# Layer 0 of a hybrid attention/convolution backbone: five stages ahead of attention become one stage over blocks of 512 tokens

## What is computed

```python
shift, scale, gate = split(silu(c) @ w_mod[0] + b_mod[0], 3)    # for the latents (c) and for the context (c_ctx)
h = rms_norm(x, g_pre[0]) * (1 + scale) + shift                # 2048 latent rows and 256 context rows
u = h @ w_in                                                   # 1024 -> 384 (q latent), 256 (kv latent), 64 (rotary key), 1024 (gate)
q  = rms_norm(cq,  g_q)  @ w_uq                                # 384 -> 8 heads x (128 + 64 rotary)
kv = rms_norm(ckv, g_kv) @ w_ukv                               # 256 -> 8 heads x (128 key + 128 value)
q_rope, k_rope = rope_2d(q_rope), rope_2d(kr)                  # latents only
```

## Time and profile before

| | us |
|---|---|
| median of 3 runs (lowest, highest) | 3414.61 (3414.49, 3419.63) |
| the profiled execution, its time | 3415.36 |
| its span, first to last instruction | 3413.6 |
| end of the last product ahead of attention, within the span | 753.3 |

### The profile page before, as it was taken

The page is one execution under the profiler, slowest core; times in us unless marked ns, Lnnn a source line. Parts: engine busy times, 40 slices in busy tenths (PEclk is TensorE's granted clock), DMA queues, the critical chain, the costliest instruction groups (busy, mean ns, idle before and its releaser), DMA issues. The chain is left out here.

```text
span 3413.6 us, 44910 instructions
## 1 busy us (share of the span) xinstructions
PE 3101.9 (91%) x15389; PEld 2570.4 (75%) x15389; DVE 1655.4 (48%) x2781; ACT 1350.1 (40%) x2896; POOL 432.8 (13%) x285
## 2 busy tenths in 40 slices
PE   7699979687999999999999999797699999997798
PEld 7588857466888787878787888686588888886677
DVE  0501134326676767676767676532533333332554
ACT  1412123345555555555555555422411111111543
POOL 1200000001111111111110111000311111112331
PEclk9799989898999999999999999999799999998899
DMA  5212133552121212121111110343322222212442
GB/s 167 82 67 74 65 108 126 174 219 90 38 66 38 67 38 66 38 66 38 62 41 53 43 38 19 136 148 116 103 70 68 70 70 70 70 51 92 158 146 101
DMA packets 216850, 285.77 MB, mean 84 GB/s; under 512 B 80560, under 2 KB 143424, under 8 KB 215488
## 3 DMA queue, kind: packets, MB, share of 16 engines
q1 hardware_dynamic: 212032, 274.76, 24.5%
q10 hardware_dynamic: 4608, 8.39, 0.7%
HBM read 185.04 MB, written 98.05 MB: 83 GB/s over the span
## 5 line engine op out<-in xcount | busy, mean ns | idle before, releaser
L988 ACT ACTIVATE at_prob<-at_S,at_nmax 128x512 f32<-128x512 f32 (+1 forms) x640 | 411.0, 658 | 373.9 <-DVE at_nmax L1102 373.9
L1125 DVE TENSOR_TENSOR at_ptlo<-at_T,at_pthi 128x512 fp32r<-128x512 f32 x576 | 396.5, 688 | 320.7 <-ACT at_pthi L1004 317.7
L1004 ACT ACTIVATE at_pthi<-at_T 128x512 fp32r<-128x512 f32 x576 | 348.9, 608 | 224.5 <-PE at_T L874 224.5
L1091 DVE TENSOR_REDUCE at_mx<-at_S 128x1 f32<-128x512 f32 (+1 forms) x640 | 393.4, 629 | 79.7 <-PE at_S L848 69.3
L874 PE MATMUL at_T<-ident,at_prob 128*128 128x128 f32 x2304 | 346.4, 273 | 1.7 <-DVE at_ptlo L1125 1.7
L874 PEld LDWEIGHTS at_T<-ident,at_prob 128*128 128x128 f32 x2304 | 278.9, 140 | 67.6 <-DVE at_ptlo L1125 13.7
L95 PE MATMUL ci_ps<-h1hi,ci_whi 128*128 128x512 f32 x768 | 299.7, 390 | 17.5 <-DVE ci_wlo L1553 17.5
L96 PE MATMUL ci_ps<-h1lo,ci_whi 128*128 128x512 f32 x768 | 299.3, 390 | 0.0
L97 PE MATMUL ci_ps<-h1hi,ci_wlo 128*128 128x512 f32 x768 | 299.3, 390 | 0.0
L843 PE MATMUL at_S<-at_khi,at_qhi 128*128 128x512 f32 (+1 forms) x640 | 250.1, 391 | 49.5 <-ACT at_prob L988 26.1
L95 PE MATMUL at_O<-at_pthi,at_vhi 128*128 128x512 f32 x576 | 272.8, 474 | 0.6 <-DVE at_og L1134 0.5
(11 more groups left out here) (201 smaller groups left out, 6293.1 us busy)
## 6 DMA issues: line engine op xcount, KB each, us to landing
at_wmod<-in_w_mod SPq DMA_DIRECT2D x32, 512.0 KB, 3.6
ci_w<-in_cv_w_in SPq DMA_DIRECT2D x24, 512.0 KB, 4.3
values<-kvu_ob SPq DMA_DIRECT2D x36, 256.0 KB, 2.0
at_kst<-k_nope SPq DMA_DIRECT2D x8, 1152.0 KB, 7.7
at_vst<-values SPq DMA_DIRECT2D x8, 1152.0 KB, 8.0
mod_w<-in_w_mod SPq DMA_DIRECT2D x16, 512.0 KB, 3.5
hid_x<-in_x SPq DMA_DIRECT2D x16, 512.0 KB, 5.2
silu_gate<-inp_ob SPq DMA_DIRECT2D x32, 256.0 KB, 2.3
```

The lines of the kernel that those rows point to most:

```text
L988: nc.scalar.activation(prob[:, j % 2, i, k], S[:, c, 0:k.stop - k.start], ACT.Exp, scale=SCALE, bias=nmax[:, i % 2:i % 2 + 1], accum_out=l ...
L1004: nc.scalar.activation(dst, T[:, (n + SLOTS * j) % 2], ACT.Copy).then_inc(s_hi, 1)
L1091: nc.vector.tensor_reduce(mx[:, i % 2, c:c + 1], S[:, c, 0:k.stop - k.start], AXX, ALU.max).then_inc(s_mx, 1)
L1125: nc.vector.tensor_tensor(ptlo[:, kt % 3], T[:, (n + SLOTS * j) % 2], pthi[:, kt % 3].bitcast(F32), ALU.subtract).then_inc(s_lo, 1)
```

## The change

`modulation`, `in_proj` and `latents` go; `front` takes their place and that of the call of `hidden` for layer 0. It is one block with no barrier inside.

- **Modulation** moves to VectorE: `w_mod` is stored transposed, `silu(c)` is broadcast over the partitions, and 32 `scalar_tensor_tensor` operations of 128x1024 with an accumulated sum give the 16 tiles for the two streams. Seven buffers of 512 KB take the weights. The first block's row statistics are done meanwhile.
- **Tokens outside, weights inside.** For each block of 512 latent tokens the 24 chunks of the list `ORDER` pass by: R0 to R5 (the latent tiles and the rotary key), G0 to G7 (the gate), U0 to U5 (two query outputs each), K0, K1 (four key outputs each), V0, V1 (four value outputs each). Each chunk (512 KB; U 384 KB) is loaded and split again for each block, in two raw buffers and three split ones, two steps ahead. The last block follows `ORDER_END`, with three chunks C3 to C5 more for the context (99 steps in all).
- **The next block's `h`** is made beside it: transposes of one eighth after each of eight steps (`T_AFTER`), into two PSUM banks; the split parts have two slots.
- **Latents stay in SBUF** and are normalised in the same block: column sums after R0 (kv) and G0 (q), roots at R1 and G1. `raw_latents` is neither written nor read.
- **Gate**: one `Silu` on ScalarE in the eviction. **Rotary**: VectorE reads PSUM itself; a `stream_shuffle` swaps the halves, three more operations combine them.

```diff
-def modulation(nc, net):
...
+RAWS, GATES, QS, KEYS, VALS = (tuple(f"{n}{i}" for i in range(k)) for n, k in (("R", 6), ("G", 8), ("U", 6), ("K", 2), ("V", 2)))
+CHUNKS = RAWS + GATES + QS + KEYS + VALS
+ORDER = ("R3 R4 R5 R0 R1 R2 G0 G1 K0 G2 K1 G3 V0 G4 V1 U0 U1 U2 G5 U3 U4 G6 U5 G7").split()
+ORDER_END = ("R3 R4 R5 R0 R1 R2 G0 C3 C4 C5 G1 G2 K0 G3 K1 V0 V1 U0 U1 G4 U2 U3 G5 U4 U5 G6 G7").split()
+T_AFTER = ("G0", "G1", "K0", "G2", "K1", "G3", "V0", "G4")
+T_AFTER_END = ("R3", "R4", "R5", "R0")
+SHUFFLE = [(i + ROPE // 4) % (ROPE // 2) for i in range(ROPE // 2)]
...
+def front(nc, net):
...
+        hhi, hlo = sb("hhi", [P, 2, KD, BLK], F32R), sb("hlo", [P, 2, KD, BLK], F32R)
+        xt = sb("x", [P, R, D])
+        tmp = sb("tmp", [P, 2, BLK])
+        wst = sb("w", [P, 2, D])
+        whi, wlo = sb("whi", [P, 3, D], F32R), sb("wlo", [P, 3, D], F32R)
...
+            load_x(0)
+            for i in range(MOD_FIRST):
+                if i >= MR:
+                    sp.wait_ge(s_mdot, 2 * (i - MR + 1))
+                sp.dma_start(mwst[:, i % MR], net.w_modr[i]).then_inc(s_mw[i % MR], 16)
+            load_w(0)
+            load_w(1)
...
+            for g, (t, name) in enumerate(seq):
+                if g + 2 < NG:
+                    sp.wait_ge(s_wlo, g + 1)
+                    load_w(g + 2)
+                if name == "R3":
+                    if t:
+                        sp.wait_ge(s_rope, 5 * t)
+                    for i in range(2):
+                        sp.dma_start(cs[:, i], net.rope_tab[i, :, t * BLK:(t + 1) * BLK]).then_inc(s_cs, 16)
+                    if t == 0:
+                        sp.wait_ge(s_T, KD)
+                        load_x(1)
+                if name == "U0" and t + 2 < len(hid):
+                    sp.wait_ge(s_T, (t + 2) * KD)
+                    load_x(t + 2)
+                if g:
+                    stores(g - 1)
+            stores(NG - 1)
...
+            for k in range(KD):
+                transposes(0, k)
+            for g, (t, name) in enumerate(seq):
+                hs, ws = t % 2, g % 3
+                pe.wait_ge(s_wlo, g + 1)
+                if name[0] in "KVU":
+                    pe.wait_ge(s_xlo, 5 * t + (5 if name[0] == "U" else KKV))
+                for o, (kind, i, e, w, ctx) in enumerate(outs[g], first_out[g]):
+                    if o >= 4:
+                        pe.wait_ge(s_evd if by_dve[o - 4] else s_eva, evicted[o - 4])
...
+                if name == "R0":
+                    column_sum(t, "kv")
+                if name == "G0":
+                    column_sum(t, "q")
+                if t == LAST:
+                    if name in T_AFTER_END:
+                        for k in range(2):
+                            transposes(t + 1, 2 * T_AFTER_END.index(name) + k)
+                    if name == "G1":
+                        column_sum(t, "c")
+                elif name in T_AFTER:
+                    transposes(t + 1, T_AFTER.index(name))
...
+            def w_high(g):
+                n = width_of(seq[g][1])
+                act.wait_ge(s_w[g % 2], 16 * (g // 2 + 1))
+                if g >= 3:
+                    act.wait_ge(s_out, first_out[g - 2])
+                nc.scalar.activation(whi[:, g % 3, 0:n], wst[:, g % 2, 0:n], ACT.Copy).then_inc(s_whi, 1)
...
+                if name == "R0":
+                    square(t, "kv")
+                if name == "R1":
+                    root(t, "kv")
+                if name == "R2":
+                    latent_high(t, "kv")
+                if name == "G0":
+                    square(t, "q")
+                if name == ("C3" if t == LAST else "G1"):
+                    root(t, "q")
+                if name == ("C5" if t == LAST else "K0"):
+                    latent_high(t, "q")
...
+                        dst, func = ob[:, b % 4, 0:w], ACT.Silu if kind == "G" else ACT.Copy
+                    nc.scalar.activation(dst, ps[:, o % 4, 0:w], func).then_inc(s_eva, 1)
...
+            def rotate(u, src, read):
+                if u >= 2:
+                    dve.wait_ge(s_rst[u % 2], 16 * (u // 2))
+                if u:
+                    dve.wait_ge(s_rope, u)
+                nc.vector.stream_shuffle(t2[:], src, SHUFFLE).then_inc(s_rob, 1)
+                nc.vector.tensor_tensor(rob[:, u % 2], src, cs[:, 0], ALU.mult).then_inc(read, 1)
+                dve.wait_ge(s_rob, 2 * u + 1)
+                nc.vector.tensor_tensor(t2[:], t2[:], cs[:, 1], ALU.mult).then_inc(s_rob, 1)
+                dve.wait_ge(s_rob, 2 * u + 2)
+                nc.vector.tensor_tensor(rob[:, u % 2], rob[:, u % 2], t2[:], ALU.add).then_inc(s_rope, 1)
...
+            for i in range(MOD_FIRST):
+                dve.wait_ge(s_mw[i % MR], 16 * (i // MR + 1))
+                if i == 2:
+                    inverse(0)
+                for s in range(2):
+                    if i:
+                        dve.wait_ge(s_mdot, 2 * i + s - 1)
+                    nc.vector.scalar_tensor_tensor(out=mjunk[:, s], in0=mwst[:, i % MR], scalar=1.0, in1=cb[:, s],
+                                                   op0=ALU.mult, op1=ALU.mult,
+                                                   accum_out=msum[:, i, s:s + 1]).then_inc(s_mdot, 1)
+            dve.wait_ge(s_mdot, 2 * MOD_FIRST)
+            nc.vector.tensor_tensor(mod[:, 0:MOD_FIRST], msum[:],
+                                    net.bm[:, 0:MOD_FIRST].unsqueeze(2).to_broadcast([P, MOD_FIRST, 2]),
+                                    ALU.add).then_inc(s_mod, 1)
+            dve.wait_ge(s_mod, 1)
+            scale_rows(nc, net, 0, 2).then_inc(s_amul, 1)
+            w_low(0)
+            for k in range(KD):
+                split_hidden(0, k)
+            w_low(1)
...
-def in_proj(nc, net, hhi, hlo):
...
-def latents(nc, net, kind):
...
-        modulation(nc, net)
-        with ExitStack() as st:
-            hhi = st.enter_context(nc.sbuf_tensor("h0hi", [P, KD, TOK], F32R))
-            hlo = st.enter_context(nc.sbuf_tensor("h0lo", [P, KD, TOK], F32R))
-            hidden(nc, net, 0, net.x, net.ctx, hhi, hlo)
-            in_proj(nc, net, hhi, hlo)
-        latents(nc, net, "q")
-        latents(nc, net, "kv")
+        front(nc, net)
```

More of the change, by code:

```diff
@@ L299, in _ @@
                             t.then_inc(s_tile, 1)
-def in_proj(nc, net, hhi, hlo):
[L304 to L389, removed]
-                act.wait_ge(s_out, o + 1)
-                if o >= 4:
-                    act.wait_ge(s_st[o % 4], 16 * (o // 4))
-                nc.scalar.activation(ob[:, o % 4, 0:width], ps[:, o % 8, 0:width], ACT.Copy).then_inc(s_free, 1)
-            def pair(i, last):
-                for r in range(2):
-                    if not (last and r):
-                        w_high(act, i, RAW + r + 1)
-                    for b in range(NBLK):
-                        o = NRAW + 4 * r + b
-                        act.wait_ge(s_out, i * 8 + (o + 1))
-                        act.wait_ge(s_free, i * 8 + (o - 1))
-                        nc.scalar.activation(sig[:, b % 2], ps[:, o % 8], ACT.Sigmoid).then_inc(s_sig, 1)
-            with act.Fori(0, HEADS // 2 - 1) as i:
-                pair(i, False)
-            pair(HEADS // 2 - 1, True)
-        @block.vector
-        def _(dve):
-            for m in range(RAW + 1):
-                w_low(dve, 0, m)
-            def pair(i, last):
-                for r in range(2):
-                    if not (last and r):
-                        w_low(dve, i, RAW + r + 1)
-                    for b in range(NBLK):
-                        o = NRAW + 4 * r + b
-                        dve.wait_ge(s_sig, i * 8 + (4 * r + b + 1))
-                        dve.wait_ge(s_st[o % 4], i * 32 + 16 * (o // 4))
-                        nc.vector.tensor_tensor(ob[:, o % 4], ps[:, o % 8], sig[:, b % 2],
-                                                ALU.mult).then_inc(s_free, 1)
-            with dve.Fori(0, HEADS // 2 - 1) as i:
-                pair(i, False)
-            pair(HEADS // 2 - 1, True)
@@ L2039, in constants @@
             rows = slice(a * half + h * half // 2, a * half + (h + 1) * half // 2)
-            tab[0, rows, :SEQ], tab[1, rows, :SEQ] = np.cos(ang[a]), np.sin(ang[a])
-    perm = np.zeros((P, P), np.float32)
-    for m in range(P):
-        if m % half < half // 2:
-            perm[m + half // 2, m] = -1.0
-        else:
-            perm[m - half // 2, m] = 1.0
+            tab[0, rows, :SEQ], tab[1, rows, :SEQ] = np.cos(ang[a]), (2 * h - 1) * np.sin(ang[a])
     mask = (np.arange(P)[:, None] // PHASES == np.arange(CCH)[None, :]).astype(np.float32)
-    return {"rope_tab": np.tile(tab, (1, 2, 1)), "perm": perm, "mask": mask, "ident": np.eye(P, dtype=np.float32)}
+    return {"rope_tab": np.tile(tab, (1, 2, 1)), "mask": mask, "ident": np.eye(P, dtype=np.float32)}
 def layout(i):
```

645 lines of the change are left out of this document (404 added, 241 removed).

## The result

The median is **3263.24 us** (3262.19 to 3265.23, 4 runs) against 3414.55 of the kernel before in the same session (3412.73 to 3419.63): ratio 0.9555, 95% interval 0.9539 to 0.9572. That is 151 us less. The forecast was 109 less, 3306, with 3280 as the lowest end. The profiled execution took 3262.19, 1.05 under the median; its span is 3260.2.

A forecast was written before the change was run, and what follows sets the result against it. TensorE, busy 91%, bounds the kernel, so the end of the last product ahead of attention decides: 80.8 + 555.2 + 8 = 644.0 instead of 753.3, 109.3 less, giving 3306 us; own range 3285 to 3325, widened to 3280 to 3345.

The forecast's parts named there:

- Lead-in: Start of the new stage: loads, 32 dots, normalising and splits, until TensorE can run without a gap from 80.8 us.
- Transposes: TensorE's transposes, now between products: 28 groups of four with one change of kind, 1.26 us each, 35.2 in all.
- Column sums: Nine float32 sums on TensorE between products at 1.20 us each (0.85 passes, 0.35 change of kind): 10.8.
- Up-projections: K, V and U on TensorE: 816 matmuls priced at 0.233 us each, 190.4; 0.227 kept for the low end.
- Stalls: TensorE's waits in the new stage: late first transposes 3, R0's column sum 3, dense context steps 2, together 8 us.
- Switches of ScalarE: Table loads between roots and `Silu`, 1.283 us each; a further drain of about 1.4 each would add 7 us.
- The tail: Stores, barrier and attention's loads after the last product: taken as unchanged.
- Rival 1: New stage: all covers hold, no stalls, accumulation free, 0.227 in the up-projections: 3286, or 3284 with faster loads; chance 0.08.
- Rivals 2 and 3: New stage's weights arrive late: short steps lengthen, 3336, chance 0.20; or landings of 12 us make it slower, 3470, chance 0.04.
- rival 2: Weights land late in short steps, at 8 us, so ScalarE's high parts wait: 28 us on U steps, 3336; chance 0.20.
- Rival 4: The stage ends earlier, but attention's start gives it back, by later stores or another clock: no change; chance 0.02.

The follow-up runs named there:

- b_moddve: Kernel before with only the modulation changed, to 32 dots on VectorE, still a stage of its own: 3415.24 us, ratio 1.0004.
- a_tr2: Kernel after with every transpose issued twice, the same piece into the same place: 3277.26 us, ratio 0.9604.
- a_dma2: Kernel after with 97 of the 99 weight chunks loaded a second time into a buffer nobody reads: 3272.34 us, ratio 0.9593.
- b_shuffle: Kernel before with only the 21 permutes on TensorE replaced by a shuffle on VectorE: 3395.17 us, ratio 0.9943.
- b_mdpad64: Kernel before with modulation as VectorE dots and 64 extra unused two-column matmuls on TensorE beside them: 3415.3 us, ratio 1.0008.
- b_mdpad32: Kernel before with modulation as VectorE dots and 32 extra unused two-column matmuls on TensorE beside them: 3394.38 us, ratio 0.9947.

## Why the prediction was right in kind and wrong in size

**Lead-in, "80.8".** Measured 69.6 for the start of the second output, 11.2 less. The first dot started at 16.9, not 18.2. "32 x 1.478 = 47.3" was the larger part of the error: a dot takes 1.15, 10.6 less in all. I took the upper bound "as accumulation always costs a read in this trace", but that read was ScalarE's, one engine's figure for another's operation. b_moddve has the same 1.15. Against this, the two normalisations took 2.4 instead of 1.9, and the dot at 27.33 took 2.04. From bias and scale on (57.2 instead of 68.0) little was gained, though the hidden splits took 1.06 instead of 1.29: "The first output, R3, is paced by those splits" was wrong. TensorE's program has all eight groups of transposes ahead of the first product; the last group starts at 63.63, and only then do the 24 products run, without a gap, past the end of the splits at 66.96. That the splits of before were slower because GpSimd worked beside them was not tested.

**Transposes, "35.2".** This is the step that failed most: "26 in 5.90, 0.227 each. Four and one change of kind are 1.26". Measured 0.48, 28 x 0.48 = 13.4: 21.8 us. Both parts of the price were wrong. The transposes of the earlier trace rows ran at half pace: about 12 of the 21.8. The same stage of the kernel before has both prices. In these windows of L294's instructions (stretch, busy PE and PEld, clock, DMA share, GB/s) the first row is the stretch of the earlier trace rows, the other two come a little later, under a recorded clock:

```profile
78.80:83.80 5.00, 5.00 (x25) 4.85 (x23) 1.00 0.75 215
98.60:101.20 2.60, 2.60 (x14) 2.60 (x14) 0.50 0.45 135
101.50:102.50 1.00, 1.00 (x12) 0.97 (x10) 1.00 0.68 123
```

From start to start these are 0.213, 0.213 and 0.11 us. The clock's record of that trace begins at 84.3; the 1.00 of the first stretch is the print of a missing record. The last stretch has the price that was needed, and I didn't look for it. Attention's 2304 transposes, too, have rows of 273 ns, where those of the earlier trace rows have 421. The other part, "0.35 the change of kind", 28 times 0.35 or 9.8 us, came from the permute's row. There TensorE starts the permute 0.50 after the product before, where 0.23 were due, with the wait put down to "issue"; it is not what a change of kind costs. In the kernel after, four transposes cost 0.48 with both changes, and four times the 0.117 of a_tr2 is 0.47.

I gave this term no lower bound, and so the range had none either: with 13.4 in place of 35.2 the forecast would have been 3284, and the measured dots would have brought it to 3274.

**Column sums, "10.8".** 0.86 each, 3.1 less: the four passes that the forecast had at 0.85, and again no 0.35 for the change of kind, neither with transposes behind the sum nor between products.

**Up-projections, "0.233".** I count them at 0.227, the low end I had kept: 5.4 less. Why the kernel before has 0.233 there (weight loads of 191 ns against 188 to 189) stays open.

**Stalls, "8".** 603.3 less 69.6 is 533.7; the work is 555.2 - 21.8 - 3.1 - 5.4 = 524.9; 8.8 are left, of which 5.9 have a name in the waits. The size was right, but by luck: of the causes that I had worked out, late transposes (3) and R0's square (3) show no wait at all, and the dense context steps (2) show 1.4: 0.78 for `fr_wlo` right behind them, at 505.41, and 0.56 for the context's column sum (`fr_sum`), at 511.71. The rest is the late loads in and beside the query steps (2.2), one eviction at 439.02 (1.5) and the rotation (0.8), where I had counted on full cover.

**Switches of ScalarE.** Each table load took 1.283, as in the earlier trace rows, and where the next activation waited for nothing else it began 0.02 later (17.10 and 1.28, then 18.40):

```profile
17.10 1.28 ACT L90 ACT_TABLE_LOAD   x1
...
18.40 0.30 ACT L90 ACTIVATE fr_rx<-fr_sx,eps 128x4 f32<-128x4 f32 x1
```

The drain that the Trainium skill (ScalarE: Activation LUTs, "What ACT_TABLE_LOAD costs") adds does not appear in this row, and the 7 us that it would have added are not there: no wait of TensorE stands at G1 in the first three blocks.

**The tail** was left as it was, rightly: 23 us in both. **Rival 1** had the right direction but too few bounds in it. **Rivals 2 and 3** did not come true, and a_dma2 with half as much traffic again did not bring them about; but rival 2's chain is there, at 2.2 us, by stores ahead on SP, as its text had said. **Rival 4**, at 0.02, was the most underrated. In the change itself it cost nothing, as attention took 1372.0, and that was luck: three of my runs (b_shuffle, b_moddve, b_mdpad64) show that this could not be counted on, since there attention gave back 8 to 18 us.

The sum of the corrections: 11.2 + 21.8 + 3.1 + 5.4 = 41.5, less 0.8 of stalls, is 40.7: 644.0 becomes 603.3. The remaining 2 us between forecast and result lie behind attention. (By its own working the forecast should have read 3305.3: 109.3 less than the median of 3414.61. The 3306 is 109.3 less than the profiled execution.)

## What to carry over

Before a price is taken from a row, look for the same operation's fastest instance in the trace and for the clock it had, and give every term a lower bound as well as an upper one: here the largest error was in the term that had none. When a change ends its stage earlier and the total doesn't move, compare the length of the unchanged stage behind it before you doubt the change: where it is a long loop, instructions added or removed ahead of it can move it by themselves, here by 14 to 18 us for 32 matmuls.

## What I had not expected of the hardware

- **Code position.** Attention, the same instructions, took 1371.9 to 1390.8 us in the twelve kernels here: 1372.6 before and 1372.0 after, 1380.2 in b_shuffle, 1386.9 in b_moddve, 1372.7 and 1390.8 with 32 and 64 idle matmuls ahead. The two longest have waits called "issue" of about 2 us on TensorE, at one instruction of the loop over heads, in each of its passes but the first. That the number of instructions ahead on TensorE decides is shown by the two padded runs. By what mechanism (how instructions are fetched after the loop's jump, say) was not shown. Why b_shuffle lost 7.6 was not tried. VectorE has such waits there, 15.1 us, also one loop pass apart, but it has 7.2 us of them in the kernel before and 9.7 in b_mdpad32, where attention is short.
- **A clock that is printed without a record.** The records of the clock begin at the first change that the trace has, at 84.3 us before and at 61.6 after, and the views print 1.00 ahead of it. Up to 83.6 the transposes of the kernel before start every 0.213, as they do from 98.6 to 101.2 under a recorded 0.50. That the clock was on its lower level is inferred from the pace. Ahead of a trace's first record I would trust the distances and not the print.
- **Reads of VectorE's accumulator** take 77 ns and run beside the next operation, where ScalarE's take 186 to 218.
- **`stream_shuffle`** of 128x512 out of PSUM takes 736 ns (16 of them), close to the 0.69 taken.
